# Hybrid diffusion step on one core: four experts chosen from two routing tiles, two of them loaded during the output stage

## The chip, the cores and the metric

One core of a Trainium2 chip (trn2) runs the whole step as one program. The metric is device microseconds (us) of one execution. The kernel before was run three times: 1116.96, 1116.96 and 1120.81 us, median 1116.96 us.

## What is computed

One inference step through one trunk layer, for 128 context tokens and 512 latent tokens of 1024 channels, in float32. A modulated RMSNorm, one input projection, four token mixers (pooling, long convolution, short convolution, attention), gates, an output projection with a gated residual, a second modulated RMSNorm, and then the part that matters here, a mixture of experts:

```python
g_prob, g_idx = lax.top_k(jax.nn.softmax(gl, axis=-1), 1)
...
e_prob, e_idx = lax.top_k(jax.nn.softmax(el_sel, axis=-1), MOE_TOP_K)
...
    hid = jax.nn.silu(a) * b * combine[:, g, :, None]
    y = y + jnp.einsum('tef,efd->td', hid, P['w_e_down'][l, g])
```

The logits `gl` pick one of four groups, `el_sel` two of its eight experts; `a` and `b` are the token rows times `w_e_gate` and `w_e_up`. So each of the 640 tokens goes to two of 32 experts, 1280 pairs in all. An expert has three weight matrices of 1 MB each (1024 x 256 twice, 256 x 1024 once), 3.15 MB. A last RMSNorm ends the step.

The routing is fixed by the inputs. Done with the reference's own formulas on its inputs, the 32 experts get 97, 87, 80, 66, 64, 64, 64, 51, 46, 46, 45, 42, 40, 40, 39, 39, 38, 38, 36, 31, 28, 28, 27, 24, 22, 22, 19, 19, 17, 12, 5 and 4 tokens. The first two tiles of 128 tokens (the context and the first 128 latent tokens) give, ordered by their counts (ties to the lower number), experts 7, 20, 3, 19, 1, 16, 22, 2, 0, 4, 18, 23, 5, 17, 13, then 29, 26, 21, 28 (15, 14, 13, 13 tokens so far; 39, 36, 31 and 19 in the end), then 24 (12 so far; 38 in the end), 31 and the rest.

## The kernel before

**Tiles and stages.** Tokens are in five tiles of 128. Up to about 740 us the mixers, gates and branches run on TensorE (PE). Then the output stage works tile by tile, with steps written out by hand in `make_steps` (L211 to L269). For tile t these are `oa`, `ob` (two halves of the output projection), `ha`, `hb` (transposes of the new residual rows), `route` (router logits) and `pos` (the place of each token in its expert's list). Every step takes the next of four PSUM buffers in turn, so PE starts a step only when the step four before it has been drained (L2010). The step `hb` of tile t also begins `oa` of tile t + 1, and for that waits for the step four before that `oa` (L2213).

After the last tile the steps `count`, `ids`, `blocks`, `perm`, `wlist`, `wperm` sort the experts by their counts and write each block's row indices.

**Ranks and blocks.** Experts are sorted by count. Experts 0 and 1 (`FIXED`, L57) get a large addend and so always have ranks 0 and 1. Ranks 0 to 7 (`WIDE`) get two blocks of 64 tokens, ranks 8 to 19 one block, ranks 20 to 31 (`PAIRED`) share a block two by two, with 32 token places each. That makes 34 blocks. `RANKS` says which rank stands at which position of the order of work.

**Weight sets.** Five sets in SBUF (`wsets`, L630) hold an expert each. The sync engine (SP) loads them (L729 to L757): experts 0 and 1 into sets 3 and 4 as soon as the last `ob` is computed (L733), then, when the ids are known (L742), positions 0 to 2. A further position's weights go into the set five before it: the first two matrices when the last block of that position has done its `up` (`gu_full`), the third when it has done its `down` (`dn_full`).

**A block** (L2375): GpSimd (POOL) gathers the token rows from DRAM (L936), PE turns them (`turn_x`), ScalarE (ACT) copies them, PE does `up` (32 matmuls, L2306, or L2335 for a shared block), ACT and VectorE (DVE) make the hidden rows, PE turns them (L1950) and does `down` (L2323, L2348), DVE scales the result (L1893), and POOL scatters it to DRAM (L940). Gathers run four blocks ahead.

**Experts with more tokens than their blocks hold** get further blocks. `fl5` (L1775) marks, per expert, a count over 32 (kept only for paired ranks) and over 64 (kept only for ranks without a second block, L1837 to L1841). `count_further` and `list_further` number them. If there is any, a loop runs behind all blocks. POOL's part of it is:

```python
            for u in range(BUFS):
                pool.wait_ge(y_sent[u], 16 * USES[u])
...
            with pool.If(n > 0):
                for i in range(2 * NT):
                    pool.indirect_dma_start(list_d, bass.IndirectOffsetOnAxis(ap=slotu[:, i:i + 1].bitcast(U32), axis=0),
                                            c_("pair")[:, i:i + 1], None).then_inc(list_out, 16)
...
                pool.wait_ge(list_out, 64 * NT)
                with pool.Fori(0, n) as i:
```

that is, ten indirect scatters of all pairs' numbers and (left out) ten of their weights; then, for each further block, four small loads of its list and weights (L984 to L988), the indices made by DVE, the gather, the block on PE and its scatter. The last stage (SP's loads of the pair rows, L767, then sums and the last norm) waits for `scatters_done`, which POOL sets behind that loop (L996). SP loads the expert's weights again for each further block (L761 to L764), from the moment that the last block's `down` is done.

Of the kernel before, what the change touches and what calls it, by code (L numbers as in the profile page):

```python
# [56 lines left out]
FIXED, WIDE, PAIRED = 2, 8, 12  # L57
LONE = EXPERTS - PAIRED

# [14 lines left out]
for _pos, _rank in enumerate(RANKS):  # L74
    if _rank < LONE:
        BLOCK += [((_pos,), b) for b in range(2 if _rank < WIDE else 1)]
    elif (_rank - LONE) % 2 == 0:
        BLOCK += [((_pos, _pos + 1), 0)]
# [29 lines left out]
def layout(items):  # L108
    at, out = 0, {}
    for name, n in items:  # L110
# [10 lines left out]
             ("keycol", 1), ("ranks", EXPERTS), ("fold", 2)])  # L121
# [5 lines left out]
def constants():  # L127
# [3 lines left out]
    def put(name, v):  # L131
        blob[:v.shape[0], CB[name][0]:CB[name][1]] = v
# [31 lines left out]
    key = (EXPERTS - 1.0 - first) + np.where(first < FIXED, 2.0 ** 20 * (FIXED - first), 0.0)  # L164
    put("key", np.tile(key, (P, 1)))
    put("keycol", key[:, None])
    put("ranks", np.tile(np.array(RANKS, f), (P, 1)))
    put("fold", (i[:, None] % 32 == np.arange(2)[None, :]) * 1.0)
# [42 lines left out]
def make_steps():  # L211
# [122 lines left out]
def build(nc, I, O):  # L334
    with ExitStack() as ctx:
# [149 lines left out]
        atplace = RP[:, 3 * D:3 * D + 2 * NT * 2 * CAP].rearrange("p (n j) -> p n j", j=2 * CAP)  # L485
# [106 lines left out]
        def ps(step):  # L592
            return pair_ps[AT[step] % 4]
# [18 lines left out]
        class Own:  # L612
# [11 lines left out]
            def link(self, ins):  # L624
# [5 lines left out]
        wsets = [(RA[:, 0:4096], RD[:, 0:D], RD[:, D:2 * D]), (RD[:, 2048:6144], RQ[:, 0:D], RQ[:, D:2 * D]),  # L630
                 (RH[:, 4096:8192], RA[:, 4096:5120], RY[:, 2816:3840]),
                 (RR[:, 0:4096], RR[:, 4096:5120], RR[:, 5120:6144]),
                 (RR[:, 6144:10240], RR[:, 10240:11264], RR[:, 11264:12288])]
# [36 lines left out]
            sem(n) for n in ("pair_weights_ready", "row_modulation", "further_weights_ready"))  # L670

# [8 lines left out]
        def _(sp):  # L680
# [52 lines left out]
            computed(sp, ("ob", NT - 1))  # L733
# [266 lines left out]
        def _(act):  # L1000
# [28 lines left out]
            for st in STEPS:  # L1029
# [122 lines left out]
                elif k == "oa":  # L1152
                    t = st[1]
                    if t == 0:
                        act.wait_ge(rows_out, 16)
                    act.wait_ge(x1_done, 2 * t + 1)
                    own.link(act.activation(junk[:, 0:HD2], x1[:, t, 0:HD2], ACT.Square, accum_out=ssq_first[:, t:t + 1]))
                    own.put(act.activation(ssq_part[:, t:t + 1], ssq_first[:, t:t + 1], ACT.Identity, bias=c_("eps"),
                                           scale=1.0 / D))
                elif k == "ob":  # L1160
                    t = st[1]
                    act.wait_ge(x1_done, 2 * t + 2)
                    own.link(act.activation(junk[:, HD2:D], x1[:, t, HD2:D], ACT.Square, accum_out=ssq[:, t:t + 1]))
# [44 lines left out]
        def _(dve):  # L1208
# [407 lines left out]
            for st in STEPS:  # L1616
# [148 lines left out]
                elif k == "early":  # L1765
                    computed(dve, st)
                    frees(dve.tensor_copy(early, ps(st)[0:EXPERTS, 0:2 * CAP]), st)
                    drained(dve, st)
                elif k == "count":
# [3 lines left out]
                    put(stt(kcol, ps(st)[0:32, 0:1], float(EXPERTS), c_("keycol", 32), ALU.mult, ALU.add))  # L1773
                    put(stt(keys, ps(st)[0:32, 32:64], float(EXPERTS), c_("key", 32), ALU.mult, ALU.add))
# [62 lines left out]
            put(ts(narrow, rank, WIDE - 0.5, None, ALU.is_gt))  # L1837
# [103 lines left out]
        def _(pe):  # L1941
# [65 lines left out]
            for n, st in enumerate(STEPS):  # L2007
# [211 lines left out]
                elif k == "route":  # L2219
                    t = st[1]  # L2220
                    drained(pe, ("shift",))
                    for kt in range(KD):
                        if kt % 4 == 0:
                            drained(pe, ("hb" if kt else "ha", t))
                        ins = mm(p_[:, 0:36], hT[:, kt, P * t:P * (t + 1)], wscaled[:, min(t, 1), kt, :], start=(kt == 0),
                                 stop=(kt == KD - 1))
                elif k == "count":
# [198 lines left out]
```

## Time and profile before

| what | us |
|---|---|
| median of three runs | 1116.96 |
| span of the profiled execution | 1117.2 |
| first weights of an expert requested | 793.8 |
| ids known, other weights requested | 808.5 |
| first block's `up` starts | 824.2 |
| last scatter issued | 1086.0 |
| pair rows requested (last stage) | 1088.8 |

The profiled execution has no time of its own beside its span; the span is 0.2 us over the median, so sums against the one hold for the other. Times below count from the span's start. "PEclk" is the granted TensorE clock as a share of full speed (1.00 is 2.4 GHz, 0.50 is 1.2 GHz). The DMA share is the mean busy share of the core's 16 DMA engines.

### The profile page before, as it was taken

The numbers are of one execution on the slowest core, as the hardware profiler recorded it, in microseconds if no ns is written. First come the engines' busy times: TensorE is split into PE (matmuls) and PEld (weight loads), VectorE is DVE, ScalarE is ACT, GpSimd is POOL, SyncE is SP. The second block draws the span as 40 slices with busy tenths as digits, with TensorE's granted clock in tenths as the row PEclk, the third lists the DMA queues.
The fourth block names the chain that finished last, engine by engine and source line by source line (L and its number), as shares of the span: only waits on it lengthen the run. The fifth ranks groups of instructions, "written<-read, shape, count | busy, mean of one in ns | idle before, by whom it ended". The sixth has DMA issues, their size and how long they took to land.

```text
span 1117.2 us, 13987 instructions
## 1 busy us (share of the span) xinstructions
PE 1010.3 (90%) x5111; PEld 623.6 (56%) x5111; DVE 567.4 (51%) x1317; ACT 209.7 (19%) x417; POOL 214.5 (19%) x282
## 2 busy tenths in 40 slices
PE   4899999999999999999999999999759999969660
PEld 2467766877555556666666666555535555435330
DVE  4466667043587667876768343155624332212226
ACT  4120001000233343333321100021110111101003
POOL 2240000010493001011111511121222233222110
PEclk9899999999999999999999999999869999979895
DMA  9861220150543343232222740310699999999957
GB/s 321 285 181 61 76 75 1 37 159 32 166 104 110 114 151 114 76 114 76 76 76 76 271 114 38 132 76 38 241 408 391 396 408 407 406 407 406 405 210 282
DMA packets 101284, 209.95 MB, mean 188 GB/s; under 512 B 8968, under 2 KB 64710, under 8 KB 101088
## 3 DMA queue, kind: packets, MB, share of 16 engines
q1 hardware_dynamic: 87984, 179.19, 44.3%
q0 software_dynamic: 13136, 29.82, 7.7%
q8 instruction: 42, 0.69, 0.3%
q14 instruction: 26, 0.21, 0.1%
q10 hardware_dynamic: 96, 0.04, 0.0%
HBM read 197.93 MB, written 18.83 MB: 194 GB/s over the span
## 4 chain that ended last, share of the span: by engine, by line
PE 76%; DMA 9%; DVE 8%; issue 3%; SPq 2%; ACT 1%; DVEq 0%; POOLq 0%; ACTq 0%
PE pair L1954 24%; PE pair L1947 11%; PE pair L2306 6%; PE pair L1992 6%; PE pair L1950 4%; DMA dft_region<-in_w_e_up 4%; PE pair L2323 4%; PE pair L1946 3%; PE pair L2112 3%; PE pair L2335 3%; PE pair L2198 2%; DMA ring_region<-in_w_gate 2%; PE pair L2089 2%; DMA hyena_region<-in_w_e_up 2%; DVE ring_region L1599 1%
## 5 line engine op out<-in xcount | busy, mean ns | idle before, releaser
L1947 PE MATMUL pair<-hT_region,ring_region 128*128 128x512 f32 x192 | 101.8, 613 | 0.0
L917 POOL TENSOR_TENSOR dft_region<-dft_region,padded_region 128x640 f32<-128x640 f32 x24 | 37.1, 1545 | 313.4 <-DVE padded_region L1521 313.4
L1954 PE MATMUL pair<-hT_region,ring_region 128*128 128x320 f32 x336 | 94.8, 435 | 0.0
L1879 DVE TENSOR_TENSOR mixer_region<-pair,mixer_region 128x128 f32<-128x128 f32 x34 | 9.9, 291 | 146.6 <-ACT mixer_region L1187 99.1
L1954 PEld LDWEIGHTS pair<-hT_region,ring_region 128*128 128x128 f32 x336 | 62.9, 190 | 28.9 <-issue 3.8
L2306 PE MATMUL pair<-ring_region,padded_region 128*64 128x256 f32 x640 | 73.5, 382 | 1.0 <-DMA ring_region<-in_w_e_up 1.0
L1992 PE MATMUL pair<-ring_region,dft_region 128*128 128x512 f32 x160 | 71.4, 596 | 0.5 <-issue 0.3
L940 POOL DMA_INDIRECT moe_pairs<-padded_region,bias_region x34 | 34.5, 1014 | 188.3 <-DVE padded_region L1893 148.2
L1946 PEld LDWEIGHTS pair<-hT_region,ring_region 128*128 128x128 f32 x192 | 36.8, 197 | 53.2 <-issue 51.4
L2306 PEld LDWEIGHTS pair<-ring_region,padded_region 128*64 128x64 f32 x640 | 44.2, 137 | 23.6 <-DMA ring_region<-in_w_e_up 1.2
L1599 DVE SCALAR_TENSOR_TENSOR ring_region<-ring_region,scT 128x256 f32<-128x256 f32 x112 | 56.9, 508 | 0.0
L1599 DVE SCALAR_TENSOR_TENSOR hyena_region<-ring_region,scT,hyena_region 128x256 f32<-128x256 f32 x112 | 55.1, 492 | 0.0
L2335 PE MATMUL pair<-dft_region,padded_region 128*32 128x256 f32 x192 | 28.7, 465 | 26.6 <-issue 18.5
L1187 ACT ACTIVATE mixer_region<-pair 128x128 f32<-128x128 f32 x34 | 9.4, 278 | 214.6 <-PE pair L2306 124.2
L1947 PE MATMUL pair<-mixer_region,ring_region 128*128 128x512 f32 x96 | 49.1, 594 | 0.0
L1992 PEld LDWEIGHTS pair<-ring_region,dft_region 128*128 128x128 f32 x160 | 29.5, 190 | 33.3 <-issue 33.3
L1893 DVE SCALAR_TENSOR_TENSOR padded_region<-pair,padded_region,hyena_region 128x512 f32<-128x512 f32 x34 | 25.5, 751 | 42.1 <-issue 35.2
L1950 PEld LDWEIGHTS pair<-constants,mixer_region 128*128 128x128 f32 x170 | 23.6, 194 | 41.3 <-issue 40.1
L1946 PE MATMUL pair<-hT_region,ring_region 128*128 128x128 f32 x192 | 39.4, 288 | 7.7 <-DMA ring_region<-in_w_gate 4.5
L1521 DVE TENSOR_TENSOR padded_region<-pair,padded_region 128x640 f32<-128x640 f32 x24 | 19.8, 823 | 43.6 <-PE pair L2198 19.5
L1954 PE MATMUL pair<-qkv_region,ring_region 128*128 128x320 f32 x144 | 41.8, 433 | 0.0
L936 POOL DMA_INDIRECT mixer_region<-h_pairs,bias_region x34 | 35.5, 1043 | 26.2 <-issue 20.2
(433 smaller groups left out, 1905.0 us busy)
## 6 DMA issues: line engine op xcount, KB each, us to landing
ring_region<-in_w_ada SPq DMA_DIRECT2D x24, 1024.0 KB, 8.2
ring_region<-in_w_gate SPq DMA_DIRECT2D x16, 1024.0 KB, 7.7
ring_region<-in_w_in SPq DMA_DIRECT2D x13, 1024.0 KB, 5.5
ring_region<-in_w_e_gate SPq DMA_DIRECT2D x12, 1024.0 KB
ring_region<-in_w_e_up SPq DMA_DIRECT2D x12, 1024.0 KB
ring_region<-in_w_e_down SPq DMA_DIRECT2D x24, 512.0 KB
hT_region<-in_w_e_gate SPq DMA_DIRECT2D x7, 1024.0 KB
hT_region<-in_w_e_up SPq DMA_DIRECT2D x7, 1024.0 KB
```

The lines of the kernel that those rows point to most:

```text
L917: pool.tensor_tensor(merged[:, dj, :], merged[:, dj, :], gtmp, ALU.add).then_inc(merged_add, 1)
L936: pool.indirect_dma_start(xg[b], None, hid_rows, bass.IndirectOffsetOnAxis(ap=idx_ap, axis=0), bounds_check=2 * NPAIR - 1, oob_is_err=Fals ...
L940: pool.indirect_dma_start(out_rows, bass.IndirectOffsetOnAxis(ap=idx_ap, axis=0), yg[b], None, bounds_check=2 * NPAIR - 1, oob_is_err=Fals ...
L1599: put(stt(sums[kind], w[:, kt, :], sc[:, kind, kt:kt + 1], sums[kind], ALU.mult, ALU.add))
L1946: mm(ps_[0:m, W0:W0 + TC], lhsT, rhs[:, 0:TC], start=start, stop=stop)
L1947: return mm(ps_[0:m, W0 + TC:1024], lhsT, rhs[:, TC:T], start=start, stop=stop)
L1950: return pe.transpose(out, in_, ident[0:n, 0:n])
L1954: ins = mm(out, weights[:, kt, :], columns[:, kt, :], start=(kt == 0), stop=(kt == KD // 2 - 1))
L1992: ins = mm(ps(("ob" if half else "oa", t))[:, 0:HD2], merged[:, kt, P * t:P * (t + 1)], w[:, kt % 2, HD2 * half:HD2 * (half + 1)], start=( ...
L2306: ins = mm(MG[u][CAP * f:CAP * (f + 1), 0:2 * P], xgT[u][:, kt % 4, kt // 4, :], wsets[s][1][:, kt, :, P * f:P * (f + 1)], start=(kt == 0) ...
L2323: ins = mm(MD[u][CAP * half:CAP * (half + 1), :], hidT[u][:, CAP * f:CAP * (f + 1)], wsets[s][2][f][:, HD2 * half:HD2 * (half + 1)], start ...
L2335: ins = mm(MG[u][at:at + HALFCAP, 0:2 * P], xgT[u][:, kt % 4, kt // 4, HALFCAP * i:HALFCAP * (i + 1)], wsets[s][1][:, kt, :, P * f:P * (f ...
```

## The change

Four experts are chosen while the output stage runs, from the counts of tiles 0 and 1: those at ranks 15 to 18 of that order. They get the large addend that experts 0 and 1 had, so that they have ranks 0 to 3 in the end; they get one block each and stand first in the order of work. `WIDE` falls from 8 to 6 and now means ranks 4 to 9; ranks 10 to 19 have one block; the twelve paired ranks stay. That makes 32 blocks. Two steps are new: `lead` (in tile 2, behind `pos` of tile 1) and `leadids` (in tile 3, behind `oa`). SP loads positions 0 and 1 as soon as the four ids are there, 2 and 3 when the last `ob` is computed, 4 when all ids are known. The sets are laid out anew, and the transposed rows for the router go to two small buffers in turn instead of `hT`.

```diff
-FIXED, WIDE, PAIRED = 2, 8, 12
+EARLY, WIDE, PAIRED = 4, 6, 12
 LONE = EXPERTS - PAIRED
+EARLY_FROM = 15
-FIRST, EVERY = 1, 5
-_double, _single = list(range(WIDE)), list(range(WIDE, LONE))
-RANKS = []
+FIRST, EVERY = EARLY, 5
+_double, _single = list(range(EARLY, EARLY + WIDE)), list(range(EARLY + WIDE, LONE))
+RANKS = list(range(EARLY))
 for _i in range(PAIRED // 2):
-    RANKS += [_single.pop(0), LONE + 2 * _i, LONE + 2 * _i + 1]
-    RANKS += [(_double if _double and (_n == 0 or _i < 3) else _single).pop(0) for _n in range(2)]
+    RANKS += [LONE + 2 * _i, LONE + 2 * _i + 1]
+    RANKS += [(_double if _double and _n < 2 else _single).pop(0) for _n in range(min(EVERY - 2, len(_double) + len(_single)))]
...
     for t in range(NT):
         s += [("oa", t)]
+        if t == 3:
+            s += [("leadids",)]
         if t:
             s += [("route", t - 1)]
         s += [("ob", t), ("ha", t)]
         if t:
             s += [("pos", t - 1)]
+        if t == 2:
+            s += [("lead",)]
         s += [("hb", t)]
...
-        wsets = [(RA[:, 0:4096], RD[:, 0:D], RD[:, D:2 * D]), (RD[:, 2048:6144], RQ[:, 0:D], RQ[:, D:2 * D]),
-                 (RH[:, 4096:8192], RA[:, 4096:5120], RY[:, 2816:3840]),
+        wsets = [(RR[:, 8192:12288], RQ[:, 0:D], RQ[:, D:2 * D]),
+                 (RA[:, 0:4096], RA[:, 4096:5120], RD[:, 5120:6144]),
                  (RR[:, 0:4096], RR[:, 4096:5120], RR[:, 5120:6144]),
-                 (RR[:, 6144:10240], RR[:, 10240:11264], RR[:, 11264:12288])]
+                 (RD[:, 0:4096], RR[:, 6144:7168], RR[:, 7168:8192]),
+                 (RH[:, 4096:8192], RD[:, 4096:5120], RY[:, 2816:3840])]
...
+            sp.wait_ge(lead_ready, 1)
+            computed(sp, ("br", 3, KD - 1))
+            for pos in range(2):
+                load_expert(early_expert(pos), pos)
             computed(sp, ("ob", NT - 1))
-            for e in range(FIXED):
-                load_expert(e, RANKS.index(e))
+            for pos in range(2, EARLY):
+                load_expert(early_expert(pos), pos)
...
             sp.wait_ge(ids_ready, 1)
-            for pos in range(SETS):
-                if RANKS[pos] >= FIXED:
-                    load_expert(expert_at(pos), pos)
+            for pos in range(EARLY, SETS):
+                load_expert(expert_at(pos), pos)
...
                 elif k in ("ha", "hb"):
                     t, k0 = st[1], 4 * int(k == "hb")
                     computed(act, st)
-                    frees(act.activation(hT[:, k0:k0 + 4, P * t:P * (t + 1)],
+                    if t >= 2 and k0 == 0:
+                        computed(act, ("route", t - 2))
+                    frees(act.activation(hturned[t % 2][:, k0:k0 + 4, :],
...
+                elif k == "lead":
+                    computed(dve, st)
+                    put(stt(lead_col, ps(st)[0:32, 0:1], float(EXPERTS), c_("keycol", 32), ALU.mult, ALU.add))
+                    frees(stt(lead_keys, ps(st)[0:32, 32:64], float(EXPERTS), c_("key", 32), ALU.mult, ALU.add), st)
+                    drained(dve, st)
+                    own.wait()
+                    link(ts(lead_keys, lead_keys, lead_col, None, ALU.is_gt))
+                    link(dve.tensor_reduce(lead_rank, lead_keys, AX.X, ALU.add))
+                    link(ts(leading, c_("iota", 32)[:, 0:EARLY], float(EARLY_FROM), lead_rank, ALU.add, ALU.is_equal))
+                    link(tt(lead_weighed, leading, c_("lead", 32), ALU.mult))
+                    link(dve.tensor_reduce(lead_more, lead_weighed, AX.X, ALU.add))
+                    put(tt(key_col, c_("keycol", 32), lead_more, ALU.add))
+                    ts(lead_diag, c_("ident", 32)[:, 0:EXPERTS], lead_more, None, ALU.mult).then_inc(lead_chosen, 1)
+                elif k == "leadids":
+                    computed(dve, st)
+                    dve.tensor_copy(lead_ids.bitcast(I32), ps(st)[0:1, 0:EARLY]).then_inc(lead_ready, 1)
+                    frees(tt(key_row, ps(st)[0:32, 32:64], c_("key", 32), ALU.add), st)
...
-            put(ts(narrow, rank, WIDE - 0.5, None, ALU.is_gt))
+            put(ts(early_narrow, rank, EARLY - 0.5, None, ALU.is_lt))
+            link(ts(narrow, rank, EARLY + WIDE - 0.5, None, ALU.is_gt))
+            put(tt(narrow, narrow, early_narrow, ALU.add))
...
+                elif k == "lead":
+                    pe.wait_ge(mask_done, 2)
+                    total = (cum[:, 1], m32[:, 1].rearrange("p g e -> p (g e)"))
+                    for i in range(2):
+                        mm(p_[0:EXPERTS, 0:1], total[i], c_("ones")[:, 0:1], start=(i == 0), stop=(i == 1))
+                    for i in range(2):
+                        ins = mm(p_[0:EXPERTS, 32:64], c_("ones")[:, 0:EXPERTS], total[i], start=(i == 0), stop=(i == 1))
+                elif k == "leadids":
+                    pe.wait_ge(lead_chosen, 1)
+                    mm(p_[0:1, 0:EARLY], c_("blk", 32).rearrange("p (b i) -> p b i", i=2)[:, 0, 0:1], leading,
+                       start=True, stop=True)
+                    ins = mm(p_[0:EXPERTS, 32:64], c_("ones")[0:EXPERTS, 0:EXPERTS], lead_diag, start=True, stop=True)
```

## Rows read from the trace of the kernel before

**Rows 1.** The page: busy time of the engines

```profile
PE 1010.3 (90%) x5111; PEld 623.6 (56%) x5111; DVE 567.4 (51%) x1317; ACT 209.7 (19%) x417; POOL 214.5 (19%) x282
```

**Rows 2.** Windows: busy us per engine, granted clock, DMA share, GB/s

```profile
760.00:780.00 20.00, 19.81 (x69) 10.63 (x69) 11.78 (x41) 4.62 (x12) 3.44 (x3) 1.00 0.14 53
795.00:1070.00 275.00, 232.81 (x1830) 126.54 (x1832) 82.59 (x232) 33.09 (x74) 70.95 (x69) 0.90 1.02 402
850.00:990.00 140.00, 139.84 (x1143) 73.15 (x1139) 45.56 (x109) 18.85 (x44) 44.64 (x44) 1.00 1.02 405
1078.00:1080.00 2.00, 2.00 (x20) 1.21 (x18) 0.03 (x1) 0.28 (x1) 0.00 (x0) 1.00 0.21 84
```

**Rows 3.** Timeline of SP: weight requests up to the first freed set

```profile
793.75 0.37 SPq L717 DMA_DIRECT2D ring_region<-in_w_e_gate  x1
...
808.46 0.41 SPq L717 DMA_DIRECT2D hT_region<-in_w_e_gate  x1
...
830.74 0.39 SPq L717 DMA_DIRECT2D hT_region<-in_w_e_gate  x1
```

**Rows 4.** Timeline of PE, ACT and POOL in the output stage, tile 2

```profile
759.94 0.39 PE L2240 MATMUL pair<-bias_region,constants 128*128 128x32 f32 x2
760.43 3.67 PE L1992 MATMUL pair<-ring_region,dft_region 128*128 128x512 f32 x8
...
762.04 0.58 ACT L1169 ACTIVATE hT_region<-pair 128x512 f32<-128x512 f32 x1
...
766.75 1.10 POOL L928 DMA_DIRECT2D h_pairs<-mixer_region  x2 [0.31 <-POOL mixer_region L924]
```

**Rows 5.** DMA of 1068.9 to 1075.8, 1076.8 to 1082.9, 1083.9 to 1086.9, 1087 to 1088.7

```profile
q0 software_dynamic: 80, 0.16, 5.8%
...
q0 software_dynamic: 80, 0.16, 6.7%
...
q0 software_dynamic: 80, 0.15, 14.0%
...
q0 software_dynamic: 80, 0.13, 20.6%
```

**Rows 6.** Timeline of POOL: the first four gathers

```profile
813.01 1.11 POOL L936 DMA_INDIRECT mixer_region<-h_pairs,bias_region  x1 [10.45 <-issue]
814.43 1.19 POOL L936 DMA_INDIRECT mixer_region<-h_pairs,bias_region  x1 [0.30 <-issue]
...
817.24 1.01 POOL L936 DMA_INDIRECT mixer_region<-h_pairs,bias_region  x1 [0.30 <-issue]
```

**Rows 7.** Timeline: the first block, the second, and late blocks

```profile
822.50 0.88 PE L1950 MATMUL pair<-constants,mixer_region 128*128 128x128 f32 x4 [1.13 <-DVE padded_region L1821]
...
824.16 6.41 PE L2306 MATMUL pair<-hT_region,padded_region 128*64 128x256 f32 x32 [0.78 <-ACT padded_region L1181]
...
830.49 1.16 PE L1950 MATMUL pair<-constants,mixer_region 128*128 128x128 f32 x5
...
831.69 0.29 DVE L1885 COPY mixer_region<-pair 128x128 f32<-128x128 f32 x1 [0.42 <-PE pair L1950]
...
839.76 0.61 PE L2335 MATMUL pair<-dft_region,padded_region 128*32 128x256 f32 x1 [8.11 <-DMA hyena_region<-in_w_e_up]
...
1075.94 3.67 PE L2306 MATMUL pair<-dft_region,padded_region 128*64 128x256 f32 x32 [1.53 <-DMA dft_region<-in_w_e_up]
...
1082.49 1.94 PE L2323 MATMUL pair<-qkv_region,mixer_region 128*64 128x512 f32 x8 [0.90 <-issue]
...
1084.52 0.75 DVE L1893 SCALAR_TENSOR_TENSOR padded_region<-pair,padded_region,hyena_region 128x512 f32<-128x512 f32 x1 [1.47 <-issue]
```

**Rows 8.** The chain that ended last: start, us, what, at its end

```profile
1086.04 2.42 DMA moe_pairs<-padded_region,bias_region
1088.50 0.04 issue
...
1088.76 0.34 SPq L769
```

More of the change, by code:

```diff
@@ L75 @@
     if _rank < LONE:
-        BLOCK += [((_pos,), b) for b in range(2 if _rank < WIDE else 1)]
+        BLOCK += [((_pos,), b) for b in range(2 if EARLY <= _rank < EARLY + WIDE else 1)]
     elif (_rank - LONE) % 2 == 0:
@@ L120 @@
              ("eps", 1), ("thr", BLOCKS), ("blk", 2 * BLOCKS), ("iota", NOV), ("half", 1), ("half_", 1), ("place", 2 * CAP), ("key", EXPERTS),
-             ("keycol", 1), ("ranks", EXPERTS), ("fold", 2)])
+             ("keycol", 1), ("ranks", EXPERTS), ("fold", 2), ("lead", EARLY)])
 CV = layout([("b_ada", 48), ("norm_mix", 8), ("b_gate", 32), ("norm_ffn", 8), ("pool_scale", 2),
@@ L163, in constants @@
     first = np.arange(EXPERTS)
-    key = (EXPERTS - 1.0 - first) + np.where(first < FIXED, 2.0 ** 20 * (FIXED - first), 0.0)
+    key = EXPERTS - 1.0 - first
     put("key", np.tile(key, (P, 1)))
@@ L167, in constants @@
     put("ranks", np.tile(np.array(RANKS, f), (P, 1)))
+    put("lead", np.tile(2.0 ** 20 * (EARLY - np.arange(EARLY)), (P, 1)))
     put("fold", (i[:, None] % 32 == np.arange(2)[None, :]) * 1.0)
@@ L484, in build @@
         cum = RB[:, 864:1056].rearrange("p (t e) -> p t e", e=EXPERTS)
-        atplace = RP[:, 3 * D:3 * D + 2 * NT * 2 * CAP].rearrange("p (n j) -> p n j", j=2 * CAP)
+        atplace = RP[:, 2944:2944 + 2 * NT * 2 * CAP].rearrange("p (n j) -> p n j", j=2 * CAP)
+        hturned = [RP[:, at:at + D].rearrange("p (k t) -> p k t", k=KD) for at in (1920, 4224)]
+        lead_ids = RB[0:1, 616:616 + EARLY]
+        leading = RB[0:EXPERTS, 624:624 + EARLY]
+        lead_rank, lead_col, lead_more, key_col = (RB[0:EXPERTS, 632 + i:633 + i] for i in range(4))
+        lead_keys, key_row = (RB[0:EXPERTS, 640 + 32 * i:672 + 32 * i] for i in range(2))
+        lead_diag = RB[0:EXPERTS, 1568:1600]
+        lead_weighed = RB[0:EXPERTS, 1600:1600 + EARLY]
+        early_narrow = RB[0:EXPERTS, 805:806]
         fin_n = RH[:, 2 * D:3 * D]
@@ L670, in build @@
             sem(n) for n in ("pair_weights_ready", "row_modulation", "further_weights_ready"))
+        lead_chosen, lead_ready = sem("early_experts_chosen"), sem("early_expert_ids_ready")
         block = ctx.enter_context(nc.Block())
@@ L731, in load_expert, with early_expert, expert_at @@
                 load_down(e, s, wd_full[s])
+            def early_expert(pos):
+                return sp.value_load(lead_ids[0:1, pos:pos + 1].bitcast(I32), min_val=0, max_val=EXPERTS - 1)
+            def expert_at(pos):
+                return sp.value_load(expert_ids[0:1, pos:pos + 1].bitcast(I32), min_val=0, max_val=EXPERTS - 1)
+            sp.wait_ge(lead_ready, 1)
+            computed(sp, ("br", 3, KD - 1))
+            for pos in range(2):
+                load_expert(early_expert(pos), pos)
             computed(sp, ("ob", NT - 1))
-            for e in range(FIXED):
-                load_expert(e, RANKS.index(e))
+            for pos in range(2, EARLY):
+                load_expert(early_expert(pos), pos)
             computed(sp, ("route", NT - 1))
             sp.wait_ge(h2_done, NT)
-            def expert_at(pos):
-                return sp.value_load(expert_ids[0:1, pos:pos + 1].bitcast(I32), min_val=0, max_val=EXPERTS - 1)
             sp.wait_ge(ids_ready, 1)
-            for pos in range(SETS):
-                if RANKS[pos] >= FIXED:
-                    load_expert(expert_at(pos), pos)
+            for pos in range(EARLY, SETS):
+                load_expert(expert_at(pos), pos)
             before = None
@@ L1768, in _ @@
                     drained(dve, st)
+                elif k == "lead":
[15 more added lines that the diff above has]
+                    frees(tt(key_row, ps(st)[0:32, 32:64], c_("key", 32), ALU.add), st)
+                    drained(dve, st)
+                    own.wait()
                 elif k == "count":
@@ L1772, in _ @@
                     nb = BLOCKS
-                    put(stt(kcol, ps(st)[0:32, 0:1], float(EXPERTS), c_("keycol", 32), ALU.mult, ALU.add))
-                    put(stt(keys, ps(st)[0:32, 32:64], float(EXPERTS), c_("key", 32), ALU.mult, ALU.add))
+                    put(stt(kcol, ps(st)[0:32, 0:1], float(EXPERTS), key_col, ALU.mult, ALU.add))
+                    put(stt(keys, ps(st)[0:32, 32:64], float(EXPERTS), key_row, ALU.mult, ALU.add))
                     frees(tt(fl5[0:32, 0:nb], ps(st)[0:32, 0:1].to_broadcast([32, nb]), c_("thr", 32), ALU.is_gt), st)
@@ L2224, in _ @@
                             drained(pe, ("hb" if kt else "ha", t))
-                        ins = mm(p_[:, 0:36], hT[:, kt, P * t:P * (t + 1)], wscaled[:, min(t, 1), kt, :], start=(kt == 0),
+                        ins = mm(p_[:, 0:36], hturned[t % 2][:, kt, :], wscaled[:, min(t, 1), kt, :], start=(kt == 0),
                                  stop=(kt == KD - 1))
+                elif k == "lead":
[10 more added lines that the diff above has]
+                    ins = mm(p_[0:EXPERTS, 32:64], c_("ones")[0:EXPERTS, 0:EXPERTS], lead_diag, start=True, stop=True)
                 elif k == "count":
```

## The prediction

> **What bounds the kernel now.** The page first: PE is busy for 1010.3 of 1117.2 us [rows 1], but an average hides stages. The windows part them [rows 2]. In the output stage (760 to 780) PE is busy for 19.81 of 20 us and the DMA engines stand nearly idle (0.14). From 795 to 1070 it is the other way round: the DMA share is 1.02 at 402 GB/s, PE is busy for 232.8 of 275 us. There is a middle (850 to 990) where both are full, but PE meets its holes before and after it, such as the 8.1 us for weights ahead of the second block [rows 7]. So the expert stage ends when the last weights have come. Only an earlier start, fewer bytes or a shorter tail behind them can move the end.
>
> The weights are requested at 793.8 for experts 0 and 1 and at 808.5 for the rest [rows 3]. Packets flow without a break from about 794.5 until about 1080 (share 0.21 in the last window that I read, 1078 to 1080 [rows 2]). That is 285.5 us for 32 experts, 8.92 us each with its gathers and scatters. Behind the last weights comes a fixed tail: last scatter at 1086.0, landed at 1088.5, pair rows requested at 1088.8 [rows 8], end at 1117.2.
>
> **The change, step by step.**
>
> *Output stage.* `lead` is four small matmuls on PE in tile 2, `leadids` two in tile 3, each of 0.2 to 0.4 us by the small matmul of `pos` (0.39) [rows 4]. A new step also moves the PSUM order. `hb` of tile 2 begins the next tile's product only when the step four before `oa` of tile 3 is drained. That was `ob` of tile 2; with `lead` in between it is `ha` of tile 2. Its drain is ACT's copy from 762.04 to 762.62, while PE begins the product at 760.43 [rows 4]. So PE waits 2.2 us, which hides `lead` itself. `leadids` adds 0.3. PE has no slack in this stage, so everything behind it comes 2.5 us later. Bounds: 0.7 (no such wait, small matmuls only) and 5 (one more wait of the same kind in tile 3, where I find none). DVE's nine small operations for `lead` fall between the norm of tile 2 and the next product, where it idles; if they were late, `leadids` would hold PE, and that is the upper bound's other half. The ACT copies of the turned rows keep their size; their new wait is for a router step two tiles back, long done.
>
> *Early loads.* `leadids` stands where PE now starts the router of tile 2, at 767.8 [rows 4], plus 2.2. With the id's copy on DVE and SP's reading of a register I take 772 for the first request. From there to the last `ob` (793.8 + 2.5) there are 24 us of idle DMA, and two experts need 2 x 8.92 = 17.8 us at most. They are fully hidden. That is the gain: up to 17.8 us of DMA work taken out of the stretch that bounds.
>
> *The hole that follows.* There are still five sets. Now positions 0 to 3 are all requested before the ids are known, and only position 4 is left to request at 808.5 + 2.5 = 811. Three experts from 797 on (positions 2, 3, 4) are in at about 797 + 3 x 8.92 = 824. SP's next request waits for set 0, which the first block's `up` frees. Its end hangs on the last tile's routing, gathers and index lists, none of which the change makes earlier: 830.7 now [rows 3], 833.2 then. So the DMA engines idle for some 9 us. In the kernel before they had two more positions to load in that time. From 833.2, plus 1 us to the first packets, 27 experts remain: 27 x 8.92 = 240.9, end at 1075.1 against 1080. The gain is 4.9 us. Bounds: 15 less 2.5 if the hole closed, 0 if the low clock of the first blocks (`up` takes 6.41 us there against 3.67 later [rows 7]) freed the next sets late as well.
>
> *Two blocks fewer.* A block takes about 6.4 us of PE, so PE saves 12.8 us. It is hidden under the DMA queue, which is the bound; the waits for weights grow by it. Nothing.
>
> *A further block.* This is the large term. What is read from the trace is that the routing counts in the front are those on the chip: the last four scatters move 0.16, 0.16, 0.15 and 0.13 MB [rows 5], and at 4096 bytes a token 38, 38, 36 and 31 tokens make 0.156, 0.156, 0.147 and 0.127. Those are ranks 16 to 19. In the kernel before every expert fits: the largest paired count is 28, the largest single count 64. After the change the chosen four are experts 29, 26, 21 and 28 with 39, 36, 31 and 19 tokens. So two of the four places go to experts with no more than 32 tokens. Nineteen experts have more than 32 tokens; the chosen hold two of them, ranks 4 to 19 hold sixteen, and one is left over: expert 24, with 38 tokens, gets rank 20, which is a paired rank with 32 places. `fl5` marks it, and the loop behind all blocks runs once. Its price, serial from the moment the last scatter has landed:
> - POOL issues twenty indirect scatters. The first gathers start 1.31 to 1.50 us apart, 4.23 for three [rows 6]; 1.35 each, 27.0. Bounds 20 (their busy time alone) and 28.
> - The last of them lands 2.42 us after its start [rows 8], 1.1 beyond its slot.
> - Four small loads at 0.55 (two took 1.10 [rows 4]) and 1.4 to land: 3.6. DVE's indices 0.2.
> - The gather, by the scatter's 2.4 [rows 8].
> - The block, at the clock of the first one, since PE has idled as before it: turn, copy and `up` from 822.50 to 830.57, 8.1 [rows 7]; silu, product, turn and copy, from 830.49 to 831.98, 1.5; `down` 1.94 at full clock [rows 7], 3.4 by the ratio of the two `up`s; the result 0.75, its 0.8 to the scatter's start, and 2.4 for that: 4.0.
>
> That is 51.3 us. The expert's weights are requested at the last `down` and need about 10 us, hidden under the 27 us of scatters; if those cost nothing it would show. Bounds: 42 (scatters at 1.0, full clock), and 67 (see below). Nothing overlaps it, for the last stage waits for `scatters_done`.
>
> What the trace cannot show is how the loop's code comes: in it no engine has taken that branch. The nearest row is POOL's step over it, 0.26 us from the landing of the scatter to SP's request [rows 8]. If each of six to seven jumps on the path (into the branch and round the loop, on POOL, PE and DVE) cost a DMA round trip as the scatter's 2.4 us, it would be 15 more; I take 0, since no row shows such a stall, and keep the 15 for the range. The Trainium skill, "Runtime: NRT & Kernel Launch", section "Instruction fetch mechanics", says that a taken branch whose target lies outside the prefetched window stalls until the page has been fetched. By that rule the sum would stand nearer to the upper end, about 1178; no row here shows it.
>
> **Sum:** 1117.2 - 4.9 + 51.3 = 1163.6 us; the 2.5 us are inside the 4.9. The median lies 0.2 lower than the span, so 1163.5.
>
> **The rivals.**
> 1. *No further block.* If the choice on the chip differs (expert 24 stands directly behind the four, one token short of the last), or I misread a mark, there is none. For it: it takes one token. Against it: the counts match to the token where the trace shows them. It decides at one expert over its places. Time 1117.2 - 4.9 = 1112.3, down to 1104.7 if the hole is hidden too. Faster or no change.
> 2. *The loop costs its jumps.* As above: 1163.5 + 15 = 1178. For it: a first run of code on five engines. Against: the step over it is cheap. This is where the page's rule would lead.
> 3. *A cheap loop.* The scatters at 1.0 and `up` at 3.67: 1163.5 - 9 = 1154.
> 4. *The hole eats the gain.* 1168.
>
> **The numbers.** A measurement of this kernel can tell about 0.5% (5.6 us) from no change. Some further block: 0.87, of that 0.55 near 1163.5, 0.14 for rival 2, 0.10 for rival 3, 0.08 for rival 4; all slower. Rival 1: 0.13, of which 0.07 beyond 5.6 us and 0.06 within. The range 1145 to 1184 takes in the bounds of the loop, and leaves out rival 1 and a few in a hundred at the top.
>
> **What would show it.** A 33rd gather and scatter, and twenty small scatters of POOL between the last of the 32 and the 33rd; some 50 us in which PE is idle but for one block at low clock. SP's first weights at about 772, a hole in the DMA share at 824 to 834, the last regular weights at about 1075. PE idle for 2 us in `hb` of tile 2. Wrong would be: 32 gathers only; or the twenty scatters under other work.

## The result and the profile after

The changed kernel took 1172.22 us (median of four runs, 1171.03 to 1174.89) against 1116.96 before; the ratio is 1.0485, 95% interval 1.0464 to 1.0507. The profiled execution has a span of 1169.5 us. The forecast was 1163.5, slower, by one further block.

The page's line of busy time says little again: PE is busy for the same time, in a longer span.

```profile
PE 1010.1 (86%) x5078; PEld 625.5 (53%) x5078; DVE 569.8 (49%) x1329; ACT 209.8 (18%) x415; POOL 235.7 (20%) x304
```

POOL's 21 us more than in [rows 1] are the first hint. The windows of the changed kernel (busy us of PE, PEld, DVE, ACT, POOL, then granted clock, DMA share, GB/s) place them:

```profile
760.00:780.00 20.00, 18.91 (x64) 9.76 (x64) 11.50 (x39) 2.58 (x8) 3.43 (x3) 0.91 0.42 153
825.00:830.00 5.00, 3.09 (x15) 2.00 (x17) 3.41 (x15) 1.88 (x2) 1.49 (x1) 0.50 0.56 220
830.00:835.00 5.00, 5.00 (x30) 3.09 (x26) 0.02 (x1) 0.28 (x1) 0.00 (x0) 0.63 0.16 49
1090.00:1100.00 10.00, 0.00 (x0) 0.00 (x0) 0.00 (x0) 0.00 (x0) 7.56 (x9) 0.50 0.02 2
1100.00:1110.00 10.00, 0.00 (x0) 0.00 (x0) 0.00 (x0) 0.00 (x0) 7.56 (x9) 0.50 0.02 0
```

From 1090 to 1110 four engines do nothing, the DMA engines next to nothing, and POOL issues. Before that the weight queue has its hole at 825 to 835. SP's timeline shows the requests around it:

```profile
773.34 0.39 SPq L734 DMA_DIRECT2D ring_region<-in_w_e_gate  x1
...
797.23 0.38 SPq L734 DMA_DIRECT2D ring_region<-in_w_e_gate  x1
...
811.56 0.38 SPq L734 DMA_DIRECT2D hyena_region<-in_w_e_gate  x1
...
834.74 0.38 SPq L734 DMA_DIRECT2D ring_region<-in_w_e_gate  x1
```

The first answers to nothing before; 797.2, 811.6 and 834.7 stand against 793.8, 808.5 and 830.7 [rows 3]. PE's timeline in tile 2 (start, us, line, operation, and idle time before it) shows the wait that the new step makes:

```profile
758.31 0.39 PE L2298 MATMUL pair<-bias_region,constants 128*128 128x32 f32 x2
...
758.84 0.23 PE L2279 MATMUL pair<-padded_region,constants 128*32 128x32 f32 x2
761.09 5.37 PE L2038 MATMUL pair<-ring_region,dft_region 128*128 128x512 f32 x8 [2.02 <-issue]
```

ACT's timeline has the copy that it waits for:

```profile
760.41 0.58 ACT L1194 ACTIVATE padded_region<-pair 128x512 f32<-128x512 f32 x1
```

In [rows 4] the product began right behind the small matmuls. Here PE idles for 2.02 us, until the copy of ACT is done at 760.99, and the product itself takes 5.37 us in place of 3.67. The chain that ended last tells the tail (start, us, what):

```profile
1080.73 7.18 DMA moe_pairs<-padded_region,bias_region
...
1088.15 1.04 issue
1089.19 0.98 POOL slot_lists L998
...
1113.45 2.69 DMA slot_weights<-padded_region,bias_region
...
1117.62 0.52 POOL bias_region L1008
...
1119.25 2.18 DMA padded_region<-slot_weights
...
1122.56 3.38 DMA mixer_region<-h_pairs,bias_region
1126.07 1.14 PE pair L1996 x4
...
1127.97 5.02 PE pair L2364 x32
...
1134.51 1.95 PE pair L2381 x8
...
1138.30 2.66 DMA moe_pairs<-padded_region,bias_region
1141.16 0.34 SPq L792
```

Between the last regular scatter at 1080.7 and SP's request for the pair rows at 1141.2 stand 60.4 us, where before there were 2.7 [rows 8]. The regular blocks end 5.3 us earlier than in [rows 8]. 57.7 - 5.3 = 52.4, and the spans differ by 52.3. The 33rd scatter moves 0.16 MB, as the 38 tokens of expert 24 would at 4096 bytes each.

The medians differ by more, 55.3 us. In every run that lists both, the time is 1.6 to 1.8 us above the span, so the profiled execution before stands for about 1118.9 us, 1.9 above its median (an estimate, since it has no time of its own), while the profiled one after (1171.15) lies 1.1 below its median. These 3.0 us are the difference between 55.3 and 52.3: it comes from which executions were profiled, and no step of the kernel has to account for it.

### The profile page after: what moved, and what is told of

It is laid out like the page before. It is cut to its first block, busy times and chain, and to the rows that moved or that the text cites. A ratio compares the mean times of both kernels' runs of the same rounds, so it can differ in the third digit from the quotient of the medians.

```text
span 1169.5 us, 14020 instructions
## 1 busy us (share of the span) xinstructions
PE 1010.1 (86%) x5078; PEld 625.5 (53%) x5078; DVE 569.8 (49%) x1329; ACT 209.8 (18%) x415; POOL 235.7 (20%) x304
## 4 chain that ended last, share of the span: by engine, by line
PE 70%; DMA 10%; DVE 8%; issue 4%; SPq 4%; POOL 2%; ACT 1%; POOLq 0%; DVEq 0%; ACTq 0%
PE pair L2000 23%; PE pair L1993 10%; PE pair L2038 6%; PE pair L2364 5%; DMA hyena_region<-in_w_e_up 4%; PE pair L1996 3%; PE pair L2158 3%; PE pair L1992 3%; PE pair L2381 2%; PE pair L2244 2%; SPq L744 2%; DMA ring_region<-in_w_gate 2%; PE pair L2135 2%; DMA dft_region<-in_w_e_down 2%; PE pair L2393 2%
## 5 line engine op out<-in xcount | busy, mean ns | idle before, releaser
L1996 PE MATMUL pair<-constants,mixer_region 128*128 128x128 f32 x165 | 36.3, 319 | 49.0 <-DMA mixer_region<-h_pairs,bias_region 47.0
L2364 PE MATMUL pair<-ring_region,padded_region 128*64 128x256 f32 x352 | 46.1, 421 | 5.3 <-DMA ring_region<-in_w_e_up 3.7
L2393 PE MATMUL pair<-hyena_region,padded_region 128*32 128x256 f32 x192 | 25.4, 423 | 23.2 <-issue 23.2
```

The lines of the kernel that those rows point to most:

```text
L1996: return pe.transpose(out, in_, ident[0:n, 0:n])
L2364: ins = mm(MG[u][CAP * f:CAP * (f + 1), 0:2 * P], xgT[u][:, kt % 4, kt // 4, :], wsets[s][1][:, kt, :, P * f:P * (f + 1)], start=(kt == 0) ...
L2393: ins = mm(MG[u][at:at + HALFCAP, 0:2 * P], xgT[u][:, kt % 4, kt // 4, HALFCAP * i:HALFCAP * (i + 1)], wsets[s][1][:, kt, :, P * f:P * (f ...
```

## The experiments

The theory: one further block, run serially behind all others, is the whole loss, and without it the change gains some 5 us. The rivals: the new sets, the step order or the block order cost something of their own; or the early loads hide nothing. Each ratio is to the kernel before, run on the same chip.

### choice13: another four experts

```diff
-EARLY_FROM = 15
+EARLY_FROM = 13
```

> The changed kernel with the four chosen from rank 13 on instead of 15 (experts 17, 13, 29, 26 with 46, 28, 39 and 36 tokens): one number differs. Then no expert is over its places and no further block runs. Theory A (the loop behind the blocks is the whole loss): 32 gathers, end at about 1112 us, 57 to 61 us below the changed kernel, ratio to before 0.99 to 1.0. Rival B (the new sets, the lost PE time and the hole in the weight queue cost something of their own too): above 1120 us.

Measured 1114.26 us, ratio 0.9959 (0.9939 to 0.9979). One number, and the loss is gone: 1.0485 less 0.9959 is 5.3% of the kernel's time, about 59 us. The last scatter starts at 1079.9 and there is no 33rd. The hole in the queue is there as in the changed kernel (windows of choice13):

```profile
825.00:830.00 5.00, 4.06 (x18) 2.65 (x20) 2.62 (x11) 1.88 (x2) 1.48 (x1) 0.50 0.60 217
830.00:835.00 5.00, 4.57 (x25) 2.73 (x22) 0.58 (x2) 0.88 (x2) 0.00 (x0) 0.72 0.14 39
```

So the gain of the rest of the change is 0.41%, 4.6 us on the 1119.7 us of the kernel before in that session.

### three_tiles: the same ranks, by more counts

The step `lead` moves behind `pos` of tile 2 and reads the counts of three tiles, `leadids` moves behind `oa` of tile 4; the ranks stay at 15 to 18. Of the edit, the part that reads the counts:

```diff
-                    pe.wait_ge(mask_done, 2)
-                    total = (cum[:, 1], m32[:, 1].rearrange("p g e -> p (g e)"))
+                    pe.wait_ge(mask_done, 3)
+                    total = (cum[:, 2], m32[:, 2].rearrange("p g e -> p (g e)"))
```

> The changed kernel with its four chosen from rank 15 on, but by the counts of three tiles instead of two (lead behind pos of tile 2, leadids behind oa of tile 4): experts 24, 26, 21 and 31 with 38, 36, 31 and 40 tokens in the end, by the reference's routing. Theory A (the loss hangs on whether sixteen or seventeen experts over 32 tokens are left for the lone blocks, not on the place from which the four are taken): none is over its places, no further block, and the time is within 4 us of choice13, ratio to before 0.993 to 1.0. Rival B (choosing middling experts at rank 15 is itself dear, for instance by the order of blocks): ratio above 1.01.

Measured 1115.65 us, ratio 0.9952 (0.9929 to 0.9975). With 384 of 640 tokens counted, rank 15 to 18 is as good as rank 13 to 16 with 256. The loss hung on which experts are chosen, not on the place in the order from which they are taken.

### before_two_further: the loop in the kernel before

```diff
-    put("thr", np.tile(np.maximum(CAP * np.arange(BLOCKS), HALFCAP) * 1.0, (P, 1)))
+    put("thr", np.tile(np.maximum(CAP * np.arange(BLOCKS), 27.5) * 1.0, (P, 1)))
```

> The kernel before, unchanged but for the mark's bound (27.5 in place of 32), so that its two paired experts with 28 tokens count as over their places and two further blocks run, computing again rows that are right. Theory A (the loop costs the same wherever it runs; from the changed kernel's trace: from the last scatter's start to the first list's load 36.9 us less the 2.7 us of a kernel without it, a round of 29 us, and a last one of 23.5 us): 87 us above the kernel before, about 1204 us, ratio 1.077. Rival B (half of the changed kernel's loss is due to its sets, its order and its output stage): under 60 us above, ratio 1.05 or less.

Measured 1206.38 us, ratio 1.0748 (1.0694 to 1.0803), against 1.077 expected: 84 us for two rounds. The loop needs nothing of the change to be dear. POOL's timeline, last regular scatter, first list scatter, first list load, and the first load of the second round:

```profile
1086.99 0.98 POOL L940 DMA_INDIRECT moe_pairs<-padded_region,bias_region  x1 [2.10 <-DVE padded_region L1893]
1094.88 0.97 POOL L975 DMA_INDIRECT slot_lists<-constants,bias_region  x1 [6.91 <-DMA moe_pairs<-padded_region,bias_region]
...
1124.65 0.57 POOL L985 DMA_DIRECT2D bias_region<-slot_lists  x1 [4.63 <-issue]
...
1154.09 0.56 POOL L985 DMA_DIRECT2D bias_region<-slot_lists  x1 [7.15 <-issue]
```

### three_further: the price of a round

The same edit of the bound in the changed kernel marks three experts (38, 28 and 28 tokens) instead of one.

> The changed kernel, but a paired expert counts as over its places from 28 tokens on (the mark's bound is 27.5 in place of 32), so that three further blocks run instead of one; the two added ones compute again rows that are right already. Theory A (the loop costs about 34 us once, above all its twenty scatters, and 24 us for each block, from the list's loads to the landed scatter): 47 to 50 us above the changed kernel, ratio to before about 1.091. Rival B (the first round is dear because its code has to come, later ones are cheap): less than 36 us above. Rival C (the next expert's weights, requested only when the last down is done, bound each round): 60 us or more above.

Measured 1233.52 us, ratio 1.0996 (1.0971 to 1.1022): 0.0511 of 1120 us, 57 us above the changed kernel, 28.6 for each added round. That is above theory A's 50 and below rival C's 60. POOL's timeline gives the rounds, first list load and scatter of each:

```profile
1123.10 0.58 POOL L1008 DMA_DIRECT2D bias_region<-slot_lists  x1 [3.95 <-issue]
...
1144.89 1.04 POOL L963 DMA_INDIRECT moe_pairs<-padded_region,bias_region  x1 [15.56 <-DVE padded_region L1939]
1153.09 0.56 POOL L1008 DMA_DIRECT2D bias_region<-slot_lists  x1 [7.16 <-issue]
...
1173.50 1.04 POOL L963 DMA_INDIRECT moe_pairs<-padded_region,bias_region  x1 [14.23 <-DVE padded_region L1939]
1181.65 0.57 POOL L1008 DMA_DIRECT2D bias_region<-slot_lists  x1 [7.11 <-issue]
...
1203.18 1.04 POOL L963 DMA_INDIRECT moe_pairs<-padded_region,bias_region  x1 [15.54 <-DVE padded_region L1939]
```

From load to scatter a round takes 21.8, 20.4 and 21.5 us, the first hardly more than the last. Ahead of its first load a round waits 1.5 to 1.6 us from the landing before it, the first round as well as the later ones. So rival B, code that has to come once, is not seen. The part that theory A had too short is the stretch from scatter to the next load: about 8.2 us, because SP has requested the next expert's 3 MB just before (1143.88 for the scatter at 1144.89). The chain has the scatter landing after 6.62 us there and after 2.65 in the last round, where nothing is requested. Theory A's 24 us left that out.

### weights_wait: nothing beside the last scatter

```diff
             with sp.If(n > 0):
+                for u in range(BUFS):
+                    sp.wait_ge(y_sent[u], 16 * USES[u])
                 with sp.Fori(0, n) as i:
```

> The changed kernel, with its further block, but SP requests the further expert's weights only when the scatters of all 32 blocks have landed, instead of at the last down. Theory A (the 3 MB of weights delay the last scatter's landing, 7.2 us against 2.4): the last scatter lands about 2.5 us after its start, the first list scatter starts 5 us earlier, and the time falls by 4 to 6 us (ratio to before about 1.044); the weights still come long before the gather. Rival B (the landing is late for another reason): no change, ratio 1.0485.

Measured 1168.42 us, ratio 1.0419 (1.0391 to 1.0446), below the changed kernel's interval: 0.0066, about 7 us. The chain confirms the part of theory A that it can (start, us, what):

```profile
1084.31 2.61 DMA moe_pairs<-padded_region,bias_region
...
1088.20 0.98 POOL slot_lists L1000
```

The landing takes 2.61 us instead of 7.18. The first list scatter starts 3.9 us behind the last regular one instead of 8.5. So 4.6 us are shown in that place. Not all of them reach the end of this execution: from the last regular scatter to SP's request for the pair rows it takes 58.9 us instead of 60.4, since the last list scatter landed after 4.47 us instead of 2.69 and the further block's `up` took 6.39 us instead of 4.99. Both differ as much between other runs (3.46 and 4.14 us, and 5.2 to 6.6 us). The 7 us of the medians are right in direction, and their size is not explained to the microsecond.

### lists_early: the twenty scatters under the blocks

```diff
+                if 8 <= n < 8 + 2 * NT:
+                    i = n - 8
+                    pool.indirect_dma_start(list_d, bass.IndirectOffsetOnAxis(ap=slotu[:, i:i + 1].bitcast(U32), axis=0),
+                                            c_("pair")[:, i:i + 1], None).then_inc(list_out, 16)
+                    pool.indirect_dma_start(weight_d, bass.IndirectOffsetOnAxis(ap=slotu[:, i:i + 1].bitcast(U32), axis=0),
+                                            signed[:, i:i + 1], None).then_inc(list_out, 16)
...
             with pool.If(n > 0):
-                for i in range(2 * NT):
...
                 pool.wait_ge(list_out, 64 * NT)
```

> The changed kernel, with its further block, but POOL issues the twenty scatters of lists and weights two by two behind the scatters of blocks 8 to 17, always, and not in the branch. Theory A (they are serial in the tail, 25 us of it): 24 to 27 us below the changed kernel, about 1147 us, if the weights of the further expert (requested at 1080 us, landed at about 1089 us) do not come to bound it. Rival B (the low priority writes only hide other waits): less than 15 us gained.

Measured 1153.19 us, ratio 1.0297 (1.0249 to 1.0345): 0.0188, 21 us less than the changed kernel, not the 24 to 27 expected. POOL's timeline shows that the tail did lose them (8.9 us from scatter to list load instead of 36.9), and that the last regular scatter comes at 1095.8 instead of 1080.7:

```profile
1095.78 0.99 POOL L963 DMA_INDIRECT moe_pairs<-padded_region,bias_region  x1 [2.10 <-DVE padded_region L1943]
1104.67 0.59 POOL L1012 DMA_DIRECT2D bias_region<-slot_lists  x1 [7.90 <-issue]
```

2.6 of those 15 us stand already in the first weight request (775.95 against 773.34), and in the tiles before it nothing has been changed: this execution, the longest of the four (1158.88 us against a median of 1153.19), ran later by chance. Most of the rest is in the window of the blocks, of lists_early and then, in the second fence, of the changed kernel:

```profile
845.00:1060.00 215.00, 184.04 (x1464) 95.70 (x1465) 58.05 (x140) 23.68 (x54) 76.01 (x75) 0.93 1.02 389
```

```profile
845.00:1060.00 215.00, 183.89 (x1482) 95.73 (x1476) 57.48 (x133) 24.61 (x56) 56.61 (x56) 0.95 1.03 407
```

The DMA engines are as busy and move 389 instead of 407 GB/s: 18 / 407 of 215 us is 9.5 us. The loss lies where the scatters are: 346 against 408 GB/s in 900 to 950 and 388 against 407 in 950 to 1000, while 845 to 900 and 1000 to 1060 agree within 1 GB/s. The scatters write 2560 pieces of four bytes, and on engines that bound the stage these cost time. By the medians less is given back: 28.0 us off the tail less the 21 gained leaves 7. They had been free in the tail only in the sense that nothing else ran there.

### choice13_load_at_ob and choice13_one_early: what the early loads are worth

```diff
-            for pos in range(2):
-                load_expert(early_expert(pos), pos)
             computed(sp, ("ob", NT - 1))
-            for pos in range(2, EARLY):
+            for pos in range(EARLY):
```

This is the first kernel: all four are requested behind `ob`. The second has 1 in place of each 2 of the changed kernel's two loops, so that one is requested early and three behind `ob`. Both choose from rank 13 on.

> As choice13, but all four chosen experts are requested when the last ob is computed (about 797 us), none during the output stage. Theory A (the weight queue bounds; only the request for the sixth expert at the end of the first up, about 834 us, and the bytes before it count): five experts from 797 on last until about 842 us, no hole, and the end comes 7 us later than in choice13, about 1119 us. Rival B (the early start hides nothing, since PE sets the end): within 2 us of choice13.

Measured 1123.11 us, ratio 1.0037 (1.0016 to 1.0057): 0.0078 or 8.7 us above choice13, 7 expected. The windows have no hole:

```profile
825.00:830.00 5.00, 3.64 (x16) 2.37 (x18) 3.00 (x14) 1.88 (x2) 1.48 (x1) 0.50 1.02 403
830.00:835.00 5.00, 4.91 (x27) 2.97 (x23) 0.29 (x1) 0.55 (x2) 0.00 (x0) 0.67 1.02 406
```

> As choice13, but only the first chosen expert is requested during the output stage, the other three when the last ob is computed. Theory A (what counts is that five experts have landed when the first up ends at about 834 us; one early expert plus four from 797 on take until 797.9 + 4 x 8.92 = 833.6): the hole of about 9 us in the queue is filled and the time is that of choice13 within 2 us, ratio to before 0.994 to 0.999. Rival B (each early expert is worth its 8.9 us): 8 to 9 us more than choice13, ratio about 1.004.

Measured 1114.29 us, ratio 0.9941 (0.9926 to 0.9955), that of choice13 within the intervals. Its windows show the hole filled as well:

```profile
825.00:830.00 5.00, 3.09 (x14) 2.19 (x15) 3.41 (x15) 1.88 (x2) 1.18 (x1) 0.50 1.03 402
830.00:835.00 5.00, 5.00 (x29) 2.96 (x25) 0.00 (x0) 0.00 (x0) 0.31 (x1) 0.58 1.03 407
```

So of the two experts loaded in the output stage the first is worth 8.7 us and the second nothing: the queue must have five experts in when the first `up` ends, and being done sooner only widens the hole.

### choice13_lead_later and choice13_lead_mid: the wait in hb

The two steps move so that no `hb` waits for the drain of `ha`; in the first the ids were to come some 15 us later, in the second some 6 (measured 16.3 and 9.9).

```diff
     for t in range(NT):
         s += [("oa", t)]
         if t == 3:
-            s += [("leadids",)]
+            s += [("lead",)]
         if t:
             s += [("route", t - 1)]
-        s += [("ob", t), ("ha", t)]
+        s += [("ob", t)]
+        if t == 3:
+            s += [("leadids",)]
+        s += [("ha", t)]
```

(This is choice13_lead_mid; `lead` is also gone from tile 2. In choice13_lead_later `leadids` stands behind `oa` of tile 4. Both have `EARLY_FROM = 13`.)

> As choice13, but the step lead stands behind oa of tile 3 and leadids behind oa of tile 4, so that no hb waits for the drain of ha; the first weights are then requested at about 788 us instead of 773. Theory A: PE keeps its 2.0 us and the low clock of the product behind them (1.7 us), everything behind the output stage comes 3 to 4 us earlier, and the later request costs nothing because the hole of 825 to 835 us takes it up: about 1108 us. Rival B (the early start at 773 is worth its 15 us): later than choice13 by 5 us or more.

Measured 1113.79 us, ratio 0.9947 (0.9923 to 0.9970). Neither theory's number: 0.0012 below choice13, within the intervals. SP's request for the sixth expert comes at 832.4 instead of 833.7, but the first request stands at 789.0 instead of 772.7, and the windows from 800 up to it have a share of 1.02 to 1.03: the queue is still full when the set comes free, so what PE saved was given back. Five experts from 789.9 on take until 834.5 by the 8.92 us of the forecast. I had called that no loss.

> As choice13, but lead stands behind oa of tile 3 and leadids behind ob of tile 3, so that no hb waits for ha's drain, and the first weights are requested at about 779 us: early enough for five experts to be in at about 825 us. Theory A: the 2 us that PE idled are saved and nothing is given back in the queue: 1.5 to 2 us below choice13, ratio to before 0.992 to 0.995. Rival B (those 2 us do not stand on the path): choice13's ratio of 0.996 or above.

Measured 1112.86 us, ratio 0.9927 (0.9910 to 0.9943), inside what theory A expected, though its interval overlaps that of choice13 (0.9939 to 0.9979). The first request stands at 782.6. PE's timeline has no idle time ahead of the product of tile 3:

```profile
762.24 0.39 PE L2299 MATMUL pair<-bias_region,constants 128*128 128x32 f32 x2
762.73 3.67 PE L2039 MATMUL pair<-ring_region,dft_region 128*128 128x512 f32 x8
```

A smaller wait is new: 0.75 us ahead of the product of tile 4, at 781.4. The profiled execution is the longest of the six and ran 2.9 us behind that of choice13 before either had reached a new step (762.24 against 759.38 at the small matmul of `pos` of tile 1). Counted from there, the last regular scatter starts after 319.4 us, in choice13 after 320.5: 1.1 us are saved, and that the move saves more is not shown.

This version has the lowest time of all: 1112.86 against 1119.97 us of the kernel before in its session, a ratio below 1 by 0.0073 or 8 us (interval 0.0057 to 0.0090), and below the changed kernel's 1.0485 by 0.0558, about 62 us. Against choice13 alone its lead is not clear of the intervals.

## Why the prediction was right, and where it was off

**Output stage.** PE waits 2.02 us where 2.2 were forecast, at the place that was named. SP's request behind the last `ob` came 3.5 us later than before, not 2.5, and even that flatters the forecast: the profiled execution after was 1.6 us ahead before its first new step (758.31 against 759.94 at the small matmul of `pos` of tile 1). Counted from there the request comes after 38.9 us, before the change after 33.8. These 5.1 us are: 2.3 for `lead` with its wait, 1.7 for the low clock of the product behind it (5.37 us for 3.67), which was not in the sum, 0.4 for `leadids`, and 0.7 between the last product and SP's request. In choice13, with no low clock there, they are 3.4.

**Early loads and the hole.** First request forecast at 772, measured 773.3; the request behind the first `up` forecast at 833.2, measured 834.7; the hole at 825 to 835. The last regular weights were to be in at 1075, and the DMA share falls from 0.32 to 0.03 at 1074. The last regular scatter was to come 4.9 us earlier and came 5.3 earlier. That this is so close is partly luck, for 1.6 of the 5.3 are the lead that this execution had at `pos`; 3.7 remain. choice13 measured the same term by itself, as 4.6 us. That the second early expert buys nothing was implied by this step ("the hole that follows") and is shown by choice13_one_early.

**Two blocks fewer.** Nothing was forecast. No kernel changed the number of blocks alone, so this is consistent (the regular part ends where the queue puts it) but not shown by itself.

**The further block.** That there would be one, from the counts, was right, and choice13 and three_tiles show it. Its price was the term that was mis-sized: 51.3 us forecast; from the landing that was assumed (1080.73 + 2.42) to the landed scatter at 1140.96 it is 57.8. By its parts:
- The last regular scatter landed after 7.2 us, not 2.4: +4.8. The forecast called the weight load hidden. It is, for itself; but it was requested at 1080.3, and from 1082 to 1090 the DMA engines are full (share 0.97 to 1.01), just when the scatter needs them. weights_wait shows it (2.61 us), and three_further shows it again in every round.
- Into the branch 1.3 us (landing to first list scatter) and ahead of the loop's first load 1.5: +2.8, forecast as 0. That is a fifth of rival 2's 15 us, and what these stretches hold stays open; the 1.5 recurs in every round of three_further (1.5 to 1.6). The Trainium skill, "Runtime: NRT & Kernel Launch", section "Instruction fetch mechanics", says that a taken branch whose target lies outside the prefetched window has to wait for that page to be fetched. The two stretches do not contradict it, but no row names a fetch.
- Twenty scatters to the last landing 26.95 (forecast 28.1). Loads 3.8 (3.6). Indices to the gather 1.1 (0.2), gather 3.5 (2.4).
- Turn to the end of `up` 6.9 (8.1) and `down` with its result 2.9 (4.2), since PE's clock rose within the block (0.50 until 1130, 0.89 in 1130 to 1133, 1.00 behind): a gain of 2.5. Some of it is this execution's luck: its `up` took 4.99 us, and in the seven further rounds of the other runs it took 5.2 to 6.6, where 6.41 was forecast.

The sum of the forecast thus ran 6.5 us low in the loop. The whole miss is 8.7 us (1172.2 against 1163.5). 5.9 of it are in the span (1169.5 against 1163.6): this 6.5, less 0.4 in the regular part and 0.2 behind the loop. The other 2.8 are that difference between the executions profiled and the medians.

**The rivals.** No further block (0.13) would have been 1112.3; choice13 is that case, 4.6 us below its own kernel before. A cheap loop fell with the scatters at 1.28 us each. Dear jumps (1178) and the eaten gain (1168) give numbers nearer to 1172.2 than the forecast does, but neither is what happened: the stretches at the branch and at the loop's head add up to 2.8 us and not 15, and the gain is there in choice13.

## What to carry to other kernels

A fallback path behind a static plan is priced by running through it once: here one expert with 38 tokens in 32 places cost 59 us, more than ten times what the rest of the change gained. When a plan reserves places by a forecast of the data, count for the real inputs how many of each size are left over, before any cycle is counted. And with a bounded queue and few buffers, an earlier start is worth only what the queue lacks when the first buffer comes free; the rest becomes a hole.

## What the runs showed of the hardware

- A scatter's landing depends on what else was just requested: 2.4 to 2.7 us alone, 6.6 to 7.2 us with 3 MB of weights requested in the microsecond around it (changed kernel, before_two_further, three_further, lists_early, weights_wait).
- Twenty scatters of 128 four-byte pieces cost their issue in an idle tail (1.28 us each on POOL) and the landing of the last (2.7 to 4.5 us), and about 9.5 us of DMA time when the DMA engines are full (389 against 407 GB/s).
- A wait of 2.0 us on PE was followed by a granted clock below full in the changed kernel (0.91 in 760 to 780, the product 5.37 us) and not in choice13, whose same product behind the same wait took 3.67 us. Of the seven traces with that wait in tile 2 four have the 5.37 us (also choice13_load_at_ob, three_further, lists_early) and three the 3.67 (also choice13_one_early, weights_wait); three_tiles, with a wait of 2.18 us one tile later, has 5.37 behind it. The seven have the same instructions up to there, so it differs by the execution; what decides it stays open.
